# Expert steps of four 32-slot chunks in three column tiles, with two weight copies, loads in expert order and 8 KB runs

## The chip, the cores and the metric

One Trainium2 chip, of which the kernel uses one core. The metric is the time of one execution on the device in microseconds (us), lower is better.

## The reference

One inference step of a two-layer backbone on 640 tokens (128 context tokens, then 512 latent tokens), 1024 wide, all in fp32. Each layer is an adaLN-modulated norm, one input projection, a pooling mixer beside multi-head latent attention, an output projection, and then a mixture of experts, which is what the change is about:

```python
scores = jax.nn.sigmoid(jnp.dot(t, router_w))
sel = scores + router_b
...
a = jnp.einsum('td,edf->tef', t, w_gate)
b = jnp.einsum('td,edf->tef', t, w_up)
act = jax.nn.silu(a) * b * gates[:, :, None]
return jnp.einsum('tef,efd->td', act, w_down)
```

Each token goes to 2 of 16 experts, so there are 1280 token rows per layer. An expert has a gate and an up matrix (1024 x 256) and a down matrix (256 x 1024), 1 MB each, 3 MB (3.146 million bytes) in all; a layer reads all 16. Worked out with the reference's own router on its inputs, the tokens of expert 0 to 15 are:

- layer 0: 75, 62, 61, 88, 132, 151, 152, 137, 29, 56, 52, 65, 54, 41, 60, 65
- layer 1: 103, 72, 81, 108, 100, 66, 83, 119, 56, 70, 40, 70, 85, 50, 93, 84

## The kernel before, in words

**Routing.** After the output projection VectorE (the `vector` block, lines 2154 to 2205) turns the top-2 mask into a list of slots sorted by expert. An expert's rows fill whole chunks of `CH = 64` slots; two chunks make a step of 128 rows. Expert 0 gets at least two chunks, so that step 0 holds expert 0 alone and its row numbers (`idx[:, 0]`, line 2164) are there before the others (`idx[:, 1:]`, line 2184). Chunks are sorted by expert, `fin[e]` is the number of steps after which expert e is done, `ech` and `eslot` hold the expert and the ring place of every chunk.

**A step** (lines 1107 to 1163 on TensorE). GpSimd gathers the step's 128 rows of the normed activations from DRAM into `xg` (line 1642). TensorE transposes them in eight pieces (1090), ScalarE and VectorE copy four pieces each to `xgT` (1445, 2191). `gate_up` multiplies them with the gate matrix and then the up matrix (1120): eight slices of the contraction, and in each of them two matmuls side by side in the array, one for each chunk, 64 columns of the array wide:

```python
for k in range(DC):
    for h in range(2):
        m = mm(dst[CH * h:CH * h + CH, 0:DE], xgT[:, k, CH * h:CH * h + CH],
               weights(h, k * 2 * DE + lo, DE), ...,
               tile_position=(0, CH * h), skip_group_check=True)
```

An fp32 matmul stands in the profile as two records (two passes). ScalarE applies silu (1467), VectorE multiplies the two (2268), TensorE transposes the product (1141) between the transposes of the next step's rows, ScalarE copies it (1470), and the down product follows (1160), again for the two chunks side by side. VectorE scales it with the gate vector (2277, 2289) and ScalarE's queue stores 128 rows to `y_rows` (1482).

**Weights.** They are loaded into a ring of `RING = 5` places of 3 MB (`load_expert`, lines 590 to 600, SP's queue), gate and up as runs of 1 KB (256 numbers of one row), down as runs of 4 KB. Expert 5 and later wait until the expert five before them is done. Chunk 0 of a step reads its weights straight from the ring, at an address held in a register; chunk 1 reads a copy (`half_gu`, `half_d`), since its expert can be another. ScalarE copies half of it (1458, 1462) and VectorE the other half (2218, 2222), three instructions of 1024 columns each on either engine. Each ring place has a semaphore, `ld_w[s]`, and TensorE, ScalarE and VectorE wait on all five of them in every step (1098, 1461, 2221), with values worked out in registers from the expert's number.

**Order around the steps.** On VectorE: rows copy, gate and up copies for the next step, the gate vector, the down copy, the scaling of the step's output. On ScalarE: silu, the two copies of the transposed product, rows copy, gate and up copies, down copy, store. Loads of experts 3 and 4 wait on SP for `r_slot` and `r_gate`, both set by VectorE after the routing (617 to 621). In the last step VectorE first builds the tables that spread the step's output to its tokens (`early_tables`, 2245), for two tiles of tokens in layer 0 and five in layer 1. Then GpSimd gathers the rows of `y_rows` for the tokens (1664), and they are added to x.

Of the kernel before, what the change touches and what calls it, by code (L numbers as in the profile page):

```python
# [52 lines left out]
CH = 64  # L53
NSTEP = 18
NSTEP_MIN = 2 * NTOK // P
NCHUNK = 2 * NSTEP
NSLOT = NSTEP * P
RING = 5
EARLY = [[0, 1], list(range(NT))]
# [29 lines left out]
def constants():  # L89
# [47 lines left out]
    put("chunk", np.tile(np.arange(NCHUNK, dtype=np.float32)[None], (P, 1)))  # L137
    least = np.tile((np.arange(NTOK // CH) * CH).astype(np.float32), (NE, 1))
    least[0, 0:2] = -1
    put("least", np.tile(least.reshape(1, -1), (P, 1)))  # L140
# [4 lines left out]
def step_kernel(nc, x_prompt, x_sample, cache_ckv, cache_krope, c, c_ctx, ada_w, ada_b, norm1_g, norm2_g, w_in, pool_w,  # L145
# [3 lines left out]
    with es:  # L149
# [123 lines left out]
        wgu = [at(6144 * s, DC, 2 * DE) for s in range(RING)]  # L273
        wd = [at(6144 * s + 4096, 2, D) for s in range(RING)]
        half_gu = flat[:, 0:4096]
        half_d = at(30720, 2 * D)

        fin = fin_s[:, :]

        def fifths(n):  # L280
            return (n * 13) >> 6
# [5 lines left out]
        def loads_of(s, e):  # L287

            return fifths(e + (RING + 1 - s if s > 0 else 1)) * 48

        def loads_before(s, l):

            return 48 + l * 48 * sum(slot_of(e) == s for e in range(NE))
# [20 lines left out]
        ecmp = view(big, rt + 1730, (NCHUNK, NE))  # L314
        ecnt = big[:, rt + 3640:rt + 3640 + NCHUNK]
        idx = big[:, 35600:35600 + NSTEP].bitcast(U32)
        ech = big[:, 35620:35620 + NCHUNK].bitcast(I32)
        n_more_s = big[:, 35680:35681].bitcast(I32)
        eslot = big[:, 35690:35690 + NCHUNK].bitcast(I32)
        is_ctx = big[:, 35740:35740 + NSTEP]  # L320
        is_ctx1 = big[:, 35760:35761]
# [18 lines left out]
        def early_rows_of(l, t, w):  # L340
# [8 lines left out]
            return flat[:, (i - 2) * D:(i - 1) * D] if i < 6 else at((i - 6) * D, D)  # L349
# [13 lines left out]
        ctx_bank = [o6, tb5]  # L363

# [29 lines left out]
        ld_w = [sem(f"ld_w{s}") for s in range(RING)]  # L394
# [10 lines left out]
        def lsem(name, count):  # L405
# [34 lines left out]
                                              "gu_mm", "dn_mm", "b_st", "w_a", "w_d")]  # L440
# [18 lines left out]
        def _(sp):  # L459
# [18 lines left out]
            def load_layer(l, expert_done):  # L478
# [19 lines left out]
                if l > 0:  # L498
                    dn_mm, b_st = by_layer[l - 1][10:12]
# [3 lines left out]
                    sp.wait_ge(dn_mm, steps)  # L503
# [25 lines left out]
            for s in range(RING):  # L529
                sp.sem_inc(ld_w[s], 48)  # L530
# [5 lines left out]
            for l in range(DEPTH):  # L536
# [51 lines left out]
                b_t, b_ta, b_td, b_sil, b_act, b_at, b_atc, b_sel, b_yd, gu_mm, dn_mm, b_st, *w_s = by_layer[l]  # L588

                def load_expert(e):  # L590

                    s = slot_of(e)
                    if e >= RING:
                        steps = sp.value_load(fin[0:1, e - RING:e - RING + 1], min_val=1, max_val=NSTEP)
                        sp.wait_ge(gu_mm, steps * 2)
                    sp.dma_start(wgu[s][:, :, 0:DE], w_gate[l, e].rearrange("(k p) n -> p k n", p=P)).then_inc(ld_w[s], 16)
                    sp.dma_start(wgu[s][:, :, DE:2 * DE], w_up[l, e].rearrange("(k p) n -> p k n", p=P)).then_inc(ld_w[s], 16)
                    if e >= RING:
                        sp.wait_ge(dn_mm, steps)
# [1725 lines left out]
```

## Time and profile before

| what | value |
|---|---|
| median of 3 runs | 1113.89 us (1113.77 to 1116.4) |
| span of the profiled execution | 1112.5 us |
| median less that span | 1.4 us |
| TensorE busy | 1058.8 us, 95% of the span |
| granted TensorE clock, mean | 0.998 of 2.4 GHz |
| bytes moved by DMA | 241.47 MB |
| expert steps | 29 (14 in layer 0, 15 in layer 1) |

The profile gives the span from the first to the last instruction. No time of its own stands beside it; the difference to the median is what lies around the span. TensorE's busy time counts overlapping matmuls once; the mean time of one matmul in a list of groups is from its start to its modelled end, and two that run side by side each count in full in their own group. Times in a timeline are from the start of the span. "Idle" stands in square brackets, with what ended it.

### The profile page before, as it was taken

To read this page: it belongs to the slowest core of one execution; us is meant where nothing else is said; L and a number is where in the kernel's file an instruction comes from. 1 tells how busy PE (TensorE), PEld (TensorE's weight loads), DVE (VectorE), ACT (ScalarE), POOL (GpSimd) and SP (SyncE) were. 2 spreads that over 40 slices of the span, in tenths; PEclk is the share of its full clock that TensorE was granted. 3 is DMA by queue.
4 is the path that set the end of the run, shared out by engine and by line. 5 is a ranking of instruction groups with operands and counts; after the bars stand their busy time and mean duration, and the time that the engine had idled before them with its cause. 6 is when DMAs were issued, how large, how long until landed. Compare 5 with 4: busy or idle time off the path is not lost.

```text
span 1112.5 us, 17990 instructions
## 1 busy us (share of the span) xinstructions
PE 1058.8 (95%) x5918; PEld 589.1 (53%) x5919; DVE 572.7 (51%) x1223; ACT 389.0 (35%) x800; POOL 204.8 (18%) x313
## 2 busy tenths in 40 slices
PE   3999999999999899999999999899999979999996
PEld 0566564555544455555546655555644445555552
DVE  0334545665345754454574545476724674534557
ACT  0332224444211244444333222454511134444540
POOL 0133456000000100100152435800000011001003
PEclk9999999999999999999999999999999999999999
DMA  9940006668801799999981000557540379999917
GB/s 351 361 138 1 1 9 238 217 222 302 331 19 40 248 378 377 381 358 366 332 289 41 1 1 0 187 194 279 207 149 38 112 260 376 381 379 380 376 78 284
DMA packets 129064, 241.47 MB, mean 217 GB/s; under 512 B 12304, under 2 KB 92192, under 8 KB 122864
## 3 DMA queue, kind: packets, MB, share of 16 engines
q1 hardware_dynamic: 115904, 194.83, 50.1%
q0 software_dynamic: 7056, 25.69, 6.3%
q10 hardware_dynamic: 6048, 20.22, 4.5%
q8 instruction: 32, 0.52, 0.2%
q14 instruction: 24, 0.20, 0.0%
HBM read 213.63 MB, written 27.10 MB: 216 GB/s over the span
## 4 chain that ended last, share of the span: by engine, by line
PE 80%; DMA 8%; DVE 3%; issue 3%; SPq 3%; POOL 1%; ACT 1%; DVEq 0%; POOLq 0%; ACTq 0%
PE bank L1120 17%; PE pair L1045 12%; PE pair L1160 9%; PE pair L762 7%; PE pair L777 6%; DMA big<-ada_w 4%; PE pair L895 4%; PE pair L794 3%; PE bank L811 3%; PE bank L931 3%; PE bank L672 3%; PE pair L1090 3%; PE bank L910 2%; PE bank L746 2%; DMA big<-y_rows,big 2%
## 5 line engine op out<-in xcount | busy, mean ns | idle before, releaser
L1120 PE MATMUL bank<-big,actT 128*64 (+1 forms) x928 | 206.3, 380 | 2.4 <-ACT actT L1445 1.9
L1120 PE MATMUL bank<-actT 128*64 128x256 f32 x928 | 206.5, 381 | 0.0
L1120 PEld LDWEIGHTS bank<-big,actT 128*64 128x64 f32 x928 | 124.7, 137 | 83.1 <-issue 26.0
L1045 PE MATMUL pair<-big,actT 128*128 128x512 f32 x320 | 142.7, 598 | 0.0
L1120 PEld LDWEIGHTS bank<-actT 128*64 128x64 f32 x928 | 124.7, 137 | 0.0
L1160 PE MATMUL pair<-big 128*64 (+1 forms) x464 | 106.0, 598 | 0.7 <-ACT big L1470 0.7
L1045 PEld LDWEIGHTS pair<-big,actT 128*128 128x128 f32 x320 | 59.0, 190 | 67.8 <-issue 67.6
L762 PE MATMUL pair<-big,actT 128*128 128x384 f32 (+1 forms) x320 | 93.6, 447 | 0.3 <-ACT actT L1218 0.2
L1988 DVE TENSOR_REDUCE mx<-pair 128x1 f32<-128x640 f32 x64 | 52.7, 823 | 72.0 <-PE pair L896 71.9
L1642 POOL DMA_INDIRECT big<-h_rows,big x29 | 27.7, 956 | 304.3 <-PE pair L1090 286.9
L762 PEld LDWEIGHTS pair<-big,actT 128*128 128x128 f32 x320 | 59.5, 190 | 29.3 <-ACT actT L1218 1.9
L895 PE MATMUL pair<-big 96*128 96x512 f32 x128 | 70.7, 634 | 1.1 <-PE bank L672 0.7
L672 PE MATMUL bank<-big,condT 128*32 128x512 f32 x384 | 53.0, 634 | 18.8 <-DMA big<-ada_w 18.7
L777 PE MATMUL pair<-actT,big 128*128 128x512 f32 (+1 forms) x256 | 70.9, 434 | 0.0
L1458 ACT ACTIVATE actT<-big 128x1024 f32 x54 | 54.1, 1049 | 37.3 <-DMA big<-w_gate 13.8
L2268 DVE TENSOR_TENSOR big<-big,bank 128x128 f32<-128x128 f32 x58 | 14.1, 284 | 102.9 <-PE bank L1120 102.9
L1631 POOL TENSOR_SCALAR ss<-big 128x1 f32<-128x1 f32 x10 | 3.0, 302 | 345.0 <-ACT big L1403 345.0
L1160 PEld LDWEIGHTS pair<-big 128*64 128x64 f32 x464 | 30.9, 136 | 55.3 <-issue 55.3
L2218 DVE COPY actT<-big 128x1024 f32 x54 | 35.0, 690 | 45.7 <-DMA big<-w_gate 17.0
L1467 ACT ACT_TABLE_LOAD x27 | 34.6, 1283 | 68.0 <-DVE big L2289 68.0
L1345 ACT ACTIVATE big<-pair,nmax 128x640 f32<-128x640 f32 x64 | 50.9, 795 | 19.0 <-DVE nmax L1991 18.6
L777 PEld LDWEIGHTS pair<-actT,big 128*128 128x128 f32 x256 | 39.1, 191 | 29.7 <-issue 29.7
(274 smaller groups left out, 1628.9 us busy)
## 6 DMA issues: line engine op xcount, KB each, us to landing
big<-ada_w SPq DMA_DIRECT2D x48, 1024.0 KB, 5.0
big<-w_gate SPq DMA_DIRECT2D x32, 1024.0 KB, 13.1
big<-w_up SPq DMA_DIRECT2D x32, 1024.0 KB, 16.3
big<-w_down SPq DMA_DIRECT2D x32, 1024.0 KB, 14.5
y_rows<-big ACTq DMA_DIRECT2D x28, 512.0 KB
big<-w_out SPq DMA_DIRECT2D x4, 2048.0 KB, 13.4
big<-mod_rows SPq DMA_DIRECT2D x16, 512.0 KB, 9.2
h_rows<-big ACTq DMA_DIRECT2D x10, 512.0 KB, 2.7
```

The costliest lines, as they stand in the source:

```text
L672: m = mm(a7[32 * j:32 * j + 32, :], condT[:, k, :], w[:, j, :], start=(k == 0), stop=(k == DC - 1), tile_position=(0, 32 * j), skip_group_ ...
L762: m = mm(in_bank(t)[:, to:to + n], actT[:, k, t * P:(t + 1) * P], vw.win_q[:, k, lo:lo + n], start=(k == 0), stop=(k == DC - 1))
L777: m = mm(pair[0][:, to:to + cols], vw.win_p[:, k, g * P:(g + 1) * P], actT[:, k, t0:t0 + cols], start=(k == 0), stop=(k == DC - 1))
L895: mm(dst[:, 0:HALF], q, vw.kT[0:QH, h, 0:HALF], start=True, stop=True)
L1045: m = mm(dst, actT[:, k, t * P:(t + 1) * P], vw.wo[n][:, k, :], start=(k == order[0]), stop=(k == order[-1]))
L1120: m = mm(dst[CH * h:CH * h + CH, 0:DE], xgT[:, k, CH * h:CH * h + CH], weights(h, k * 2 * DE + lo, DE), start=(k == 0), stop=(k == DC - 1) ...
L1160: m = mm(pair[1][CH * h:CH * h + CH, j * HALF:(j + 1) * HALF], acT[:, k, CH * h:CH * h + CH], weights(h, 4096 + k * D + j * HALF, HALF), s ...
L1345: f(prob[un % 4][:, :, :], score_bank(un)[:, 0:NLK * P].rearrange("p (k n) -> p k n", n=P), ACT.Exp, bias=nmax[:, un % 2:un % 2 + 1], scal ...
L1458: return f(pieces(half_gu), pieces(slot[:, 0:4096]), ACT.Copy)
L1467: f(sil, tb4[:, 0:DE], ACT.Silu).then_inc(b_sil, 1)
L1988: link(v.tensor_reduce(mx[:, un % 2:un % 2 + 1], score_bank(un)[:, 0:NLK * P], AX.X, ALU.max))
L2218: return v.tensor_copy(pieces(half_gu), pieces(slot[:, 0:4096]))
```

## The change

- A chunk has 32 slots, a step four chunks. Every expert gets at least one chunk, every expert with an odd number at least two, expert 0 at least four. The steps are worked as three column tiles, `TILES = [(0, 64), (64, 32), (96, 32)]`: two chunks of one expert that stand next to each other share the 64-slot tile, the other two chunks get 32 slots each. Which chunks these are is worked out on VectorE (`tile_e`), and slots are moved within their step so that the pair comes first.
- The 64-slot tile reads the ring. The tile at 64 reads a copy made by ScalarE alone, the tile at 96 one made by VectorE alone. Each copy is six pieces of 1024 columns a step, in three buffers per engine; one semaphore, `used`, counts the pieces that TensorE has used (six a step).
- Step 0 is one tile of 128 slots, read from the ring, with no copies. TensorE makes the list of the other rows (`list_rows`) inside step 0, after its first piece.
- `load_expert` loads gate and up as 8 KB runs (partition p takes rows 8p to 8p+7); the normed rows are written in the matching order (`by_row`, a stride of 128 numbers). Each of gate, up and down has one semaphore, and a load waits until the same matrix of the expert before has landed.
- The buffers that receive the last gathers of layer 1 move, and one wait of GpSimd in the last step of layer 1 goes.
- The loop is peeled: step 0, then the loop, then the last step.

```diff
-CH = 64
-NSTEP = 18
+CH = 32
+NSTEP = 19
+TILES = [(0, 64), (64, 32), (96, 32)]
...
     least = np.tile((np.arange(NTOK // CH) * CH).astype(np.float32), (NE, 1))
-    least[0, 0:2] = -1
+    least[:, 0] = -1
+    least[1::2, 1] = -1
+    least[0, 0:FIRST_CHUNKS] = -1
...
                 def load_expert(e):
                     s = slot_of(e)
                     if e >= RING:
                         steps = sp.value_load(fin[0:1, e - RING:e - RING + 1], min_val=1, max_val=NSTEP)
-                        sp.wait_ge(gu_mm, steps * 2)
-                    sp.dma_start(wgu[s][:, :, 0:DE], w_gate[l, e].rearrange("(k p) n -> p k n", p=P)).then_inc(ld_w[s], 16)
...
+                        sp.wait_ge(used, used_in(steps, 1))
+                    if e > 0:
+                        sp.wait_ge(ld_wg, landed(l, e - 1))
+                    sp.dma_start(wg[s], w_gate[l, e].rearrange("(p k) n -> p (k n)", k=DC)).then_inc(ld_wg, 16)
...
+                def products(n, land, place, first):
+                    tiles = [(0, P)] if first else TILES
+                    pe.wait_ge(b_ta, n + 1)
+                    pe.wait_ge(b_td, n + 1)
+                    for i in range(4):
+                        if first and i == 1:
+                            list_rows()
+                        weights = weights_of(n, i, land, place, first)
+                        dst = (tb4, tb5)[i // 2]
+                        for k in range(4 * (i % 2), 4 * (i % 2) + 4):
+                            for c, (lo, m_) in enumerate(tiles):
+                                m = mm(dst[lo:lo + m_, 0:DE], xgT[:, k, lo:lo + m_], weights(c, k % 4 * DE, DE),
+                                       start=(k == 0), stop=(k == DC - 1), tile_position=(0, lo), skip_group_check=True)
+                        m.then_inc(used, 1)
...
```

ScalarE's step, and VectorE's:

```diff
+                def step(n, first, last):
+                    if not first:
+                        part = part_place(n)
+                        part_copy_w(n, part, 3)
+                    act.wait_ge(used, used_at(n, 1))
                     f(sil, tb4[:, 0:DE], ACT.Silu).then_inc(b_sil, 1)
+                    if not first:
+                        part_copy_w(n, part, 4)
+                        part_copy_w(n, part, 5)
                     for k in range(2):
                         act.wait_ge(b_at, n * 2 + (k + 1))
                         f(acT[:, k, :], (o6, a7)[k][:, 0:P], ACT.Copy).then_inc(b_atc, 1)
...
+                    rows_copy(n + 2)
+                    part = part_place(n + 1)
+                    for i in range(3):
+                        part_copy_w(n + 1, part, i)
```

```diff
+                def step(n, first, last):
                     if last:
                         early_tables()
+                    if not first:
+                        part = part_place(n)
+                        for i in range(3, NPIECES):
+                            part_copy_w(n, part, i)
                     ve.wait_ge(b_sil, n + 1)
```

GpSimd's gathers at the end of a layer:

```diff
-                        if i == (2 if l == 0 else 6):
-                            reached(dn_mm, n_steps)
+                        if i == 2 and l == 0:
+                            reached(used, used_in(n_steps, 5))
```

The routing chain on VectorE gets 15 more instructions before the slots are known and 13 more between them and `r_slot`.

## Rows read from the trace of the kernel before

**Rows 1.** The page, parts 1 and 2: busy times; 40 slices of the span

```profile
PE 1058.8 (95%) x5918; PEld 589.1 (53%) x5919; DVE 572.7 (51%) x1223; ACT 389.0 (35%) x800; POOL 204.8 (18%) x313
...
DMA  9940006668801799999981000557540379999917
```

**Rows 2.** The page, part 5: gathers of rows, one for each step

```profile
L1642 POOL DMA_INDIRECT big<-h_rows,big x29 | 27.7, 956 | 304.3 <-PE pair L1090 286.9
```

**Rows 3.** Chain of waits, in order of time: start, length, what

```profile
400.32 6.97 PE bank L1120 x64
408.66 3.65 PE pair L1160 x16
412.32 7.10 PE bank L1120 x64
```

**Rows 4.** Stretches: busy PE, PEld, DVE, ACT, POOL, PE clock, DMA share, GB/s

```profile
12.00:27.00 15.00, 8.38 (x52) 2.10 (x44) 0.76 (x1) 1.15 (x2) 0.76 (x2) 0.89 1.00 417
387.40:557.40 170.00, 168.10 (x1253) 95.02 (x1254) 81.08 (x149) 76.98 (x108) 14.21 (x15) 1.00 1.03 366
908.50:1091.40 182.90, 180.26 (x1343) 101.74 (x1344) 90.02 (x168) 83.31 (x118) 17.32 (x19) 1.00 0.91 325
400.00:538.00 138.00, 137.74 (x1036) 77.84 (x1036) 64.72 (x104) 65.83 (x91) 10.33 (x11) 1.00 1.05 373
```

**Rows 5.** Timeline of TensorE from one step into the next: start, length, what

```profile
406.90 0.38 PE L1120 MATMUL bank<-big,actT 128*64 x1
406.92 0.38 PE L1120 MATMUL bank<-actT 128*64 128x256 f32 x1
407.23 0.55 PE L1090 MATMUL pair<-cst,big 128*128 128x128 f32 x3
...
411.71 0.60 PE L1160 MATMUL pair<-big 128*64 x2
412.29 0.42 PE L1120 MATMUL bank<-big,actT 128*64 x1
...
412.55 0.38 PE L1120 MATMUL bank<-big,actT 128*64 x1
```

**Rows 6.** The page, part 5: gate and up copies on ScalarE and VectorE

```profile
L1458 ACT ACTIVATE actT<-big 128x1024 f32 x54 | 54.1, 1049 | 37.3 <-DMA big<-w_gate 13.8
...
L2218 DVE COPY actT<-big 128x1024 f32 x54 | 35.0, 690 | 45.7 <-DMA big<-w_gate 17.0
```

**Rows 7.** Timelines around step 0 of layer 0: VectorE, GpSimd, SP, TensorE

```profile
379.45 0.24 DVE L2167 TENSOR_TENSOR big<-big,mask 128x80 f32<-128x80 f32 x1
...
384.80 0.75 DVE L2187 TENSOR_REDUCE big<-big 128x36 f32<-128x576 f32 x1
...
386.54 0.69 DVE L2191 COPY actT<-pair 128x512 f32<-128x512 f32 x1 [0.98 <-PE pair L1090]
...
387.26 0.95 POOL L1642 DMA_INDIRECT big<-h_rows,big  x1 [6.08 <-PE pair L1090]
...
390.86 0.37 SPq L596 DMA_DIRECT2D big<-w_gate  x1
...
395.43 0.55 PE L1090 MATMUL pair<-cst,big 128*128 128x128 f32 x3 [0.86 <-DMA big<-h_rows,big]
```

**Rows 8.** Timeline of VectorE in the last step of layer 0, then of layer 1

```profile
548.61 0.14 DVE L2247 TENSOR_SCALAR big<-fin 128x1 f32<-128x1 int32 x1
...
550.43 0.49 DVE L2257 TENSOR_TENSOR part_s<-part_s,bias_s 128x128 f32<-128x128 f32 x2
...
1081.00 1.22 DVE L2289 TENSOR_TENSOR big<-pair,big 128x1024 f32<-128x1024 f32 x1
1082.13 0.14 DVE L2247 TENSOR_SCALAR big<-fin 128x1 f32<-128x1 int32 x1
...
1086.33 0.28 DVE L2257 TENSOR_TENSOR big<-big 128x128 f32<-128x128 f32 x1
```

**Rows 9.** Timeline of VectorE: the last normed rows of layer 0

```profile
371.29 1.29 DVE L2151 SCALAR_TENSOR_TENSOR big<-big,rs 128x1024 f32<-128x1024 f32 x1 [0.59 <-POOL rs L1632]
```

More of the change, by code:

```diff
@@ L393, in step_kernel @@
         mod_st = sem("mod_st")
-        ld_w = [sem(f"ld_w{s}") for s in range(RING)]
+        ld_wg, ld_wu, ld_wd = sem("ld_wg"), sem("ld_wu"), sem("ld_wd")
         y_fill = sem("y_fill")
@@ L1107, in products @@
[L1107 to L1123 removed]
+                    land = pe.value_load(eland[0:1, bass.ds(n, 1)], min_val=16, max_val=landed(DEPTH - 1, NE - 1))
@@ L1133, in products @@
-                    return weights
-                def rest(n, last, weights):
-                    w_a, w_d = w_s
+                    for i in range(4):
[8 more added lines that the diff above has]
+                        m.then_inc(used, 1)
@@ L1139, in turn_act, with rest @@
+                def rest(n, land, place, first, last):
+                    tiles = [(0, P)] if first else TILES
                     def turn_act(k):
@@ L1170, in _ @@
                 n_more = pe.value_load(n_more_s[0:1, 0:1], min_val=NSTEP_MIN - 1, max_val=NSTEP - 1)
-                rest(0, False, weights)
+                rest(0, land_0, place_0, True, False)
                 def step(n, last):
-                    rest(n, last, products(n))
+                    land, place = load_place(n)
+                    products(n, land, place, False)
+                    rest(n, land, place, False, last)
                 with pe.Fori(1, n_more) as i:
@@ L1499, in _ @@
                 act.wait_ge(op_mm, L(op_mm) + 2 * NT)
[L1500 to L1504 removed]
+                act.sem_inc(w_a, NPIECES - 1)
                 rows_copy(1)
                 act.wait_ge(y_fill, 16 * (NSTEP - NSTEP_MIN))
[L1507 to L1508 removed]
+                step(0, True, False)
                 n_more = act.value_load(n_more_s[0:1, 0:1], min_val=NSTEP_MIN - 1, max_val=NSTEP - 1)
[L1510 to L1514 removed]
+                with act.Fori(1, n_more) as i:
+                    step(i, False, False)
+                step(n_more, False, True)
         @block.gpsimd
@@ new lines, in _ @@
+                link(red(ecnt, ecmp, AX.X, ALU.add))
+                ts(fin, ends, float(FIRST_CHUNKS - 1), None, ALU.add)
+                link(ts(ecnt, ecnt, float(NE - 1), None, ALU.min))
+                ve.wait_ge(r_pe1, L(r_pe1) + 2)
+                v.tensor_copy(idx[:, 1:NSTEP], pair[1][:, 1:NSTEP]).then_inc(r_idx, 1)
+                ts(is_ctx, pair[1][:, 0:NSTEP], float(SEQ), None, ALU.is_lt).then_inc(b_yd, 1)
+                e0, e1, e2, e3 = (ecnt.rearrange("p (n j) -> p n j", j=FIRST_CHUNKS)[:, :, j] for j in range(4))
@@ L2289, in step @@
                     tt(yb, pair[1][:, :], yb, ALU.mult).then_inc(b_yd, 1)
-                with ve.Fori(0, n_more) as i:
-                    step(i, False)
-                step(n_more, True)
+                    part_copy_w(n + 1, part, 2)
+                step(0, True, False)
+                with ve.Fori(1, n_more) as i:
+                    step(i, False, False)
+                step(n_more, False, True)
             l = DEPTH - 1
```

331 lines of the change are left out of this document (173 added, 158 removed).

## The prediction, made blind

> **What bounds the kernel now.** I read the busy times of the page first: TensorE is busy for 95% of the span, and the DMA digits are 9 or near it in slices 15 to 20 and again in the second mixture of experts [rows 1]. So either could be the limit there. The chain of waits settles it: from step to step it is only TensorE's own matmuls, 7.1 us of gate and up (L1120), 3.6 us of down (L1160), and the transposes between [rows 3]. From the gate and up product at 400.32 to that at 412.32 is 12.0 us; between the stretches of the next view it is 12.1 us a step. The gathers count 29 steps [rows 2], 14 in layer 0 (170.0 us) and 15 in layer 1 (182.9 us) [rows 4]. No step is longer than another but the first of a layer, where TensorE waits 0.86 us for gathered rows [rows 7]. Yet the DMA share of steady steps in layer 0 is 1.05 at 373 GB/s [rows 4]: the queues are full all the time and the weights come just in time. A change that shortens the steps' total has to bring the bytes sooner as well.
>
> **Fewer steps.** With the reference's token counts, 64-slot chunks give 28 and 29 chunks, so 14 and 15 steps, which is what the gathers show. Chunks of 32 with the new minima give 48 and 49, four to a step: 12 and 13. Four steps of 12.1 us go: -48.4 us, if a step costs what it did.
>
> **What a step costs.** Its arithmetic on TensorE is as before if the three tiles run side by side as the two do now: the two chunks' matmuls start 0.02 us apart and each takes 0.38 [rows 5]. I take that; the other case is the first rival. At the seam TensorE's next product starts 0.58 us after the last pair of the down product [rows 5], which streams for 0.43 (eight pairs in 3.65 us, the last 0.60 long, [rows 3, 5]): 0.15 us are left, in which its queue works out the five waits on `ld_w`. One wait replaces them, so up to 23 x 0.15 = 3.4 us come back. Against it stand the copies. ScalarE now copies six pieces of 1.05 us instead of three, VectorE six of 0.69 [rows 6], 6.3 and 4.1 us a step. By ScalarE's order (silu, pieces 4 and 5, then the transposed product) the latter comes some 8.5 us after the step's start, when the down product wants it: up to 0.2 us late, 4.6 us over 23 steps. I take the two at nothing together, and both ends for the range. VectorE has over 1 us to spare for each piece.
>
> **The bytes.** From the load of expert 3 at 390.9 [rows 7] thirteen experts remain (40.9 MB), and a gather and a store (1.05 MB together) for each step. Before, at 373 GB/s, 54.5 MB take 146 us and end at 537; expert 15 is needed at 545. After, `r_slot` and `r_gate` come about 5 us later, expert 15 is needed at 387.4 + 11 x 12.1 + 2 = 522.5, and 52.4 MB at 373 GB/s would end at 536.5: 14 us late. The 8 KB runs decide. While the kernel starts, `ada_w` is loaded in runs of 8 KB, at 417 GB/s [rows 4]; two thirds of the weights would go at that rate, and 52.4 MB at some 410 take 128 us and end at 523.7. I take 0.5 us a layer for what is late, 1 us in all; the ends are 0 and 14 us a layer. The Trainium skill (DMA: Bandwidth & Descriptors, Where 436 GB/s comes from) holds that the core's share of HBM, about 358 GB/s, binds such loads; by that rule the longer runs would bring nothing and the 14 us a layer stand. The rows of this trace are above it at either run length.
>
> **Step 0 of each layer.** It starts no later: what step 0 needs comes ahead of the added instructions. The gather for step 1 does. Before, it starts at 387.26, when the transposes free the buffer [rows 7]. After, VectorE's comparison and reduction over 76 chunks instead of 36 (0.75 us each for 576 numbers, so 1.4 each for 1216, [rows 7]) follow the rows copy, and TensorE makes the list only after the first piece (389.2 to 389.8): the list's copy comes at about 390.6, 3.4 us later. The fewer loads in flight give perhaps 1.4 us back: +2.0 us for each layer, 0.3 to 3.5. The fifteen added routing instructions (some 0.25 us where one waits for the last, [rows 7]) take about 2.5 us, beside the transposes and the first piece.
>
> **The last step of each layer.** VectorE builds the tables from 1082.13 to 1086.6 in layer 1, 4.5 us, and in 2.3 us in layer 0 [rows 8]. Now they stand ahead of its pieces 3 to 5, of which TensorE wants piece 3 5.1 us after the step starts. VectorE is free about 3.1 us after it (the output's scaling, 1.22 us, [rows 8], and piece 2), then come the tables, two register loads and the copy: 9.2 us in layer 1, 7.2 in layer 0. TensorE waits 4.0 and 2.0 us. In layer 1 some 1.2 us hide in waits of the final additions: +4.8 in all, 2 to 7.
>
> **The rest.** The normed rows are written at a stride of 512 bytes; the last such instruction, 1.29 us, stands before the last mask [rows 9]. The trace has none with such a stride: at least 0, at most twice the time there and in its half before, 2 us a layer. I take 0, since VectorE's time here goes by the count of its numbers (1.29 us for 1024, 0.75 for 576, [rows 7, 9]). The gathers at the end of layer 1 lose a wait, but VectorE's additions bound that stretch: 0. One count per matrix keeps at most three transfers in flight; three of 1 MB cover 7 us at 417 GB/s: 0.
>
> **Sum:** -48.4 + 1 + 4 + 4.8 = -38.6. The profiled span, 1112.5, becomes 1073.9; the median of the runs is 1.4 above its span: **1075.3 us**. Own range: -3.4 with the low ends (0, 0.6 and 2) gives 1065, taken as 1063 for the rounding of 25 steps; the high ends (7, 7, 4.6, 4 for the strides, and half of the 28 us of late bytes) give 1102.
>
> **Rival 1, slower: the tiles of 64 and 32 columns exclude each other.** Wherever the width of the matmuls changes, the next starts later than where it stays: the last pair of L1120 starts at 406.90 and 406.92, and pairs follow each other every 0.21 us (64 records in 7.10, [rows 3]), but the full-width transpose behind it starts after 0.31 [rows 5]: 0.10 us for one change. Where that is a wait for the array to be empty, the 64-column tile can't share it with the 32-column ones. Then the 16 products of gate and up and the 4 double ones of down each run twice in turn: +10.3 us a step, 40 changes of 0.10 us, and 1.5 us for weights not loaded ahead (the first pair takes 0.26 instead of 0.21, [rows 5]): +15.8, times 23 steps (step 0 has one tile) +363. The waits of the first and last steps hide in it (-8): 1430 us. It decides from 1.7 us a step (38.6 over 23), so one change of 0.10 in each of 20 groups would do. For it: the delay at every change. Against: every change in this trace is between tiles that overlap in the array, which must wait anyway; tiles that don't overlap start together. The Trainium skill has the rule (TensorEngine Tiling (Array Packing), Key Properties): changing the tiling mode, not just the tile, drains TensorE. By it this rival holds; the 0.10 us agree, but no row mixes widths in disjoint columns.
>
> **Rival 2, slower: they overlap, but each change costs its 0.10 us.** 3.8 us a step, 23 steps: 1075 + 87 = 1162.
>
> **Rival 3: the longer runs bring nothing,** and expert 15 is 14 us late in each layer. 1075.3 - 1 + 28 = 1102 us. For it: the rate rose in part because the start has no gathers. Against: 417 beside 373 GB/s.
>
> **Chances.** As forecast 0.58; rival 3 0.06; within 0.3% (3.3 us, about what a measurement of this kernel tells from no change), by several waits together, 0.02; rival 1 0.30; rival 2 0.04. Both signs hold much, so the range goes from 1063 to the end of rival 1, 1440; the likeliest case's own is 1063 to 1102. Faster 0.64, same 0.02, slower 0.34.
>
> **What would show it.** 25 gathers; steady steps of 12.0 to 12.3 us; three matmuls of a group starting within 0.03 us of each other, against 0.5 us for rival 1. `w_gate` and `w_up` landing sooner with a DMA share under 1 and no copies waiting for them after the tenth step; the second gather some 3 us later; a wait of TensorE for VectorE's piece 3 in the last steps. A step of 14 us or more would make the prediction wrong at its root.

## The result, and the profile after

The changed kernel takes **1429.27 us** (1427.26 to 1432.43, 4 runs), the kernel before in the same comparison 1115.03 us (1113.77 to 1116.4, 4 runs): 1.2814 times the time, 95% interval 1.2788 to 1.284. The forecast was 1075.3 us and faster. What came is rival 1, which gave 1430 us with a chance of 0.30.

The page's parts 1 and 2, its gathers, and the two stretches of the experts (columns as in [rows 4]):

```profile
PE 1370.2 (96%) x6402; PEld 590.8 (41%) x6403; DVE 624.4 (44%) x1312; ACT 404.2 (28%) x810; POOL 201.7 (14%) x309
...
DMA  9900166850597324563440015661069444644115
...
L1676 POOL DMA_INDIRECT big<-h_rows,big x25 | 23.9, 955 | 549.1 <-PE pair L1129 511.3
```

```profile
388.40:705.70 317.30, 313.34 (x1483) 93.35 (x1484) 98.86 (x182) 87.45 (x114) 13.33 (x13) 1.00 0.52 194
1060.10:1405.80 345.70, 342.07 (x1613) 102.24 (x1614) 110.03 (x204) 95.81 (x126) 20.13 (x21) 1.00 0.46 172
```

The change does what it says: 25 gathers for 29 [rows 2]. The DMA queues, full before [rows 4], are half empty. The two stretches got longer, 317.3 us for 170.0 and 345.7 for 182.9, and TensorE is busy all through them (313.3 us for 168.1, and 342.1 for 180.3). VectorE and ScalarE, which now copy more, grew by some 10 to 20 us in each and stand idle for most of it. The chain of waits shows each step alike:

```profile
404.10 18.11 PE bank L1165 x96
423.57 7.94 PE pair L1192 x24
431.51 18.11 PE bank L1165 x96
```

From one gate and up product (L1165) to the next it is 27.4 us where it was 12.1 on average (12.0 in [rows 3]): 18.1 for 7.1, and the down product (L1192) 7.9 for 3.65. Between them it is 1.36 us (422.21 to 423.57), as before. The timeline of TensorE inside a product shows where that goes (start, length; "x3" are three records in a row):

```profile
412.52 0.40 PE L1165 MATMUL bank<-actT 128*32 128x256 f32 x1
412.53 0.40 PE L1165 MATMUL bank<-big,actT 128*32 128x256 f32 x1
412.76 0.38 PE L1165 MATMUL bank<-actT 128*32 128x256 f32 x1
412.77 0.95 PE L1165 MATMUL bank<-big,actT 128*32 128x256 f32 x3
413.65 0.40 PE L1165 MATMUL bank<-actT 128*32 128x256 f32 x1
413.66 0.40 PE L1165 MATMUL bank<-big,actT 128*32 128x256 f32 x1
```

The same in the weight loads (PEld):

```profile
413.08 0.19 PEld L1165 LDWEIGHTS bank<-big,actT 128*64 128x64 f32 x2 [0.41 <-issue]
413.65 0.11 PEld L1165 LDWEIGHTS bank<-actT 128*32 128x32 f32 x1 [0.39 <-issue]
```

The two tiles of 32 columns start 0.01 us apart, as close as the two of 64 in [rows 5]. The tile of 64 is the last two of the "x3" records of 412.77, which the weight loads of 64 columns date: it starts at 413.08, and nothing of another width does until 413.65. A group takes 1.13 us (412.52 to 413.65); two equal tiles take 0.43.

What the change made late is small beside it. TensorE's waits in step 0 of layer 0 (us in all, times, the longest):

```profile
PE pair L1129 <- DMA big<-h_rows,big: 2.9, 1, 2.9
PE bank L1165 <- ACT actT L1481: 0.9, 1, 0.9
PE bank L1175 <- DVE big L2337: 0.3, 1, 0.3
```

### The profile page after: what moved, and what is told of

Its sections match the earlier page's. It is cut to its first block, busy times and chain, and to the rows that moved or that the text cites. A ratio compares the mean times of both kernels' runs of the same rounds, so it can differ in the third digit from the quotient of the medians.

```text
span 1425.4 us, 19416 instructions
## 1 busy us (share of the span) xinstructions
PE 1370.2 (96%) x6402; PEld 590.8 (41%) x6403; DVE 624.4 (44%) x1312; ACT 404.2 (28%) x810; POOL 201.7 (14%) x309
## 4 chain that ended last, share of the span: by engine, by line
PE 87%; DMA 5%; DVE 4%; issue 2%; SPq 1%; ACT 1%; POOL 0%; DVEq 0%; ACTq 0%; POOLq 0%
PE bank L1165 29%; PE pair L1192 13%; PE pair L1081 10%; PE pair L798 6%; PE pair L813 5%; DMA big<-ada_w 4%; PE pair L931 3%; PE bank L708 3%; PE pair L830 3%; PE bank L847 3%; PE bank L967 3%; PE bank L946 2%; PE pair L1129 2%; PE bank L782 1%; DMA big<-h_rows,big 1%
## 5 line engine op out<-in xcount | busy, mean ns | idle before, releaser
L1165 PE MATMUL bank<-big,actT 128*64 (+2 forms) x1168 | 341.8, 399 | 1.7 <-ACT actT L1481 1.7
L1165 PE MATMUL bank<-actT 128*32 128x256 f32 x1104 | 229.0, 391 | 0.0
L1497 ACT ACTIVATE actT<-big 128x1024 f32 x138 | 145.5, 1056 | 270.0 <-PE bank L1165 155.7
L1192 PE MATMUL pair<-big 128*32 128x512 f32 (+2 forms) x384 | 191.9, 612 | 0.7 <-ACT big L1511 0.7
L1165 PEld LDWEIGHTS bank<-big,actT 128*64 128x64 f32 (+2 forms) x1168 | 107.4, 129 | 164.8 <-issue 161.2
L2289 DVE COPY big<-big 128x1024 f32 x92 | 63.6, 691 | 180.1 <-PE bank L1165 173.0
L1165 PEld LDWEIGHTS bank<-actT 128*32 128x32 f32 x1104 | 51.8, 108 | 141.6 <-issue 141.6
L1192 PE MATMUL pair<-actT,big 128*32 128x512 f32 x184 | 96.2, 605 | 0.0
L1192 PEld LDWEIGHTS pair<-big 128*32 128x32 f32 (+2 forms) x384 | 33.4, 125 | 65.6 <-issue 65.6
L2357 DVE TENSOR_TENSOR big<-pair,big 128x1024 f32<-128x1024 f32 x23 | 28.1, 1224 | 68.4 <-PE pair L1192 68.4
L1381 ACT ACTIVATE big<-pair,nmax 128x640 f32<-128x640 f32 x64 | 50.8, 794 | 18.9 <-DVE nmax L2026 18.5
```

What stands on the lines that cost most here:

```text
L1165: m = mm(dst[lo:lo + m_, 0:DE], xgT[:, k, lo:lo + m_], weights(c, k % 4 * DE, DE), start=(k == 0), stop=(k == DC - 1), tile_position=(0, l ...
L1192: m = mm(pair[1][lo:lo + m_, j * HALF:(j + 1) * HALF], acT[:, k, lo:lo + m_], weights(c, j * HALF, HALF), start=(k == 0), stop=(k == 1), t ...
L1381: f(prob[un % 4][:, :, :], score_bank(un)[:, 0:NLK * P].rearrange("p (k n) -> p k n", n=P), ACT.Exp, bias=nmax[:, un % 2:un % 2 + 1], scal ...
L1497: f(parts[1][i % 3], slot[:, i * PIECE:(i + 1) * PIECE], ACT.Copy).then_inc(w_a, 1)
L2289: v.tensor_copy(parts[2][i % 3], slot[:, i * PIECE:(i + 1) * PIECE]).then_inc(w_d, 1)
```

## The experiments

In the timings of a run, the kernel before stood beside it on the same chip (medians 1114 to 1117 us). Single profiles of kernels that are alike outside the expert steps differ by up to 6 us in the start and the end, so terms of a few us are read from the stretches of the experts, first product to last.

### Which of the costs of the mix it is

**Four tiles of one width.** The changed kernel, with a list of tiles of TensorE's own (source of the weights, first column, columns) in place of `TILES`:

```diff
+MM_TILES = [(0, 0, 32), (1, 32, 32), (1, 64, 32), (2, 96, 32)]
...
-                            for c, (lo, m_) in enumerate(tiles):
+                            for c, lo, m_ in tiles:
```

> The changed kernel with the pair of chunks as two tiles of 32 columns, so that all four tiles of a step have one width. The tile at 32 reads ScalarE's copy, so slots 32 to 63 are multiplied with the weights of the third chunk's expert: the time is meant, the output of those slots is left wrong. Theory (tiles of different widths exclude each other, tiles of one width don't): the four stream side by side, gate and up take 7.1 us a step again, down 3.65, the step 12.1 to 12.5, the whole 1075 to 1090 us. Rival A (it is the number of matmuls and weight loads that costs: six records of a group take 1.13 us, so eight take 1.5): the step about 34 us, the whole about 1580 us. Rival B (tiles of 32 columns are slow by themselves): no better than now, 1429 us.

Measured: 1092.5 us (1091.41 to 1094.34), 0.978 of before (0.974 to 0.9821). The timeline inside a product (the first line is the tile that reads the ring, the second the other three):

```profile
952.81 0.38 PE L1166 MATMUL bank<-big,actT 128*32 x1
952.82 0.39 PE L1166 MATMUL bank<-actT 128*32 128x256 f32 x3
953.03 0.38 PE L1166 MATMUL bank<-big,actT 128*32 x1
953.03 0.39 PE L1166 MATMUL bank<-actT 128*32 128x256 f32 x3
```

Four tiles start within 0.02 us, and every 0.21 us. Splitting the wide tile in two, with more matmuls, took 337 us off. Both rivals fall: it is neither the number of matmuls nor the narrow tiles. The time is 2.5 us above the theory's own range, which the next run takes up.

**Two tiles of 64.** The same list with `[(0, 0, 64), (1, 64, 64)]`.

> The changed kernel with the third and fourth chunk as one tile of 64 columns on ScalarE's copy (slots 96 to 127 are multiplied with the third chunk's weights, so that part of the output is left wrong; VectorE's copies are still made and waited for). Theory: with one width the rest of the sum is measured as it was forecast: steps of 12.0 to 12.3 us and 1063 to 1102 us, 1075 by the sum. Rival (the copies, the step's waits or the loads of the changed kernel cost as well, hidden now behind the long steps): steps of over 12.5 us with TensorE waiting in them, over 1102 us.

Measured: 1080.38 us (1078.13 to 1080.71). One thing has to be added: with wrong weights in layer 0 the tokens of layer 1 choose other experts, which fill 12 steps there, not 13 (24 gathers in all; the run with four tiles has 25). One step more makes it 1092.7, the four tiles' time. So two widths of tile give one time. Both are 17 us above the forecast, and all steps but the first of the loop are 12.2 us or longer. The theory's range holds, and its steps of 12.0 to 12.3 us hold for most of layer 1; but the rival has a point too: something of the changed kernel costs TensorE time beyond the widths, though less than the rival said (over 12.5 us a step, over 1102 us).

**Fewer changes of width.** The changed kernel's three tiles, in another order:

```diff
-                        for k in range(4 * (i % 2), 4 * (i % 2) + 4):
-                            for c, (lo, m_) in enumerate(tiles):
+                        for cs in ([0], [1, 2])[:len(tiles)]:
+                            for k, c in [(k_, c_) for k_ in range(4 * (i % 2), 4 * (i % 2) + 4) for c_ in cs if c_ < len(tiles)]:
+                                lo, m_ = tiles[c]
...
```

> The changed kernel with the matmuls of a piece in another order: all of the 64-column tile first, then all of the two 32-column ones; the same matmuls with two changes of width in a piece where there were eight (two where there were four in a piece of the down product). Theory (exclusion and a drain at each change): the exclusion stays, 14.4 us for gate and up at least, but 24 + 4 changes with some 0.1 us and weights not loaded ahead go: gate and up 14.5 to 15 us, down 7.3 to 7.6, the step 23 to 24, the whole 1330 to 1350 us. Rival (only changes of width cost, tiles of both widths can overlap): gate and up about 8 us, the whole about 1115 us. Rival (exclusion alone costs and changes nothing): 1429 us as now.

Measured: 1343.87 us (2 runs), 1.2024 of before, as the theory said. From its chain of waits:

```profile
431.69 14.89 PE bank L1166 x96
...
447.95 7.40 PE pair L1194 x24
455.35 14.89 PE bank L1166 x96
```

The step is 23.66 us. A step of the changed kernel has 40 changes of width, this one 12 (two in each of six pieces): 27.42 - 23.66 = 3.76 us for 28 changes, 0.134 us for each, with the weights that aren't loaded ahead. The two products give the same price by themselves: 18.11 - 14.89 us for 24 changes, 7.94 - 7.40 for four. What is left above a step of equal tiles (11.87, below) is 11.8 us, of which 12 changes are 1.6; **10.2 us is the exclusion**, each group run twice in turn.

**The mix alone, in the kernel before.** Chunk 1 as two tiles of 32 columns on the same copy:

```diff
+MM_TILES = [(0, 0, 64), (1, 64, 32), (1, 96, 32)]
...
-                            for h in range(2):
+                            for h, a, w_ in MM_TILES:
...
```

> The kernel before with chunk 1 worked as two tiles of 32 columns on the same copy (the same products, nothing else changed). Theory: the mix of widths alone makes the steps long: each of the 29 steps takes 27.4 us instead of 12.1, 1114 + 29 x 15.3 = 1558 us, less a few hidden waits, 1545 to 1560. Rival (the length comes from the new waits, the three copies or the counting of pieces): 1114 us, or up to 1130 with a few more instructions to issue.

Measured: 1558.57 us (2 runs), inside the theory's 1545 to 1560; the rival falls. Its chain shows the same two numbers, with nothing else of the change in it:

```profile
442.76 18.11 PE bank L1121 x96
462.24 7.94 PE pair L1161 x24
```

### What else the forecast had missed

**ScalarE's piece 3.** In the run with two tiles of 64, TensorE waits for ScalarE's copies 15 times, 5.6 us in all. Part of the chain of waits into such a wait ("ACTq" is the queue of ScalarE at work on loads of registers, issues and jumps):

```profile
942.03 1.23 DVE big L2358
...
943.41 0.35 ACTq L1524
...
944.10 0.28 ACTq L1488
...
944.71 0.36 ACTq L1489
...
945.52 1.07 ACT actT L1498
946.58 0.13 issue
946.71 1.95 PE bank L1166 x16
```

VectorE's scaling of the output (L2358) is done at 943.3. Then ScalarE issues the store (L1524), jumps to the head of its loop, loads two registers (L1488, L1489), and only at 945.52 copies piece 3. TensorE goes on at 946.71. The next run moves that copy behind the store:

```diff
-                        part_copy_w(n, part, 3)
...
                     act.dma_start(y_rows[bass.ds(n * P, P), :], yb).then_inc(b_st, 16)
+                    part_copy_w(n + 1, part, 3)
```

> The kernel with two tiles of 64 columns (1080 us), and ScalarE copies piece 3 of the next step at the end of the step, behind the store, with the registers it has, in place of behind the loop's jump and two register loads. In the trace of two tiles of 64, ScalarE's piece 3 starts 1.8 us after the store was issued and ends just after TensorE wants it; steady steps of layer 1 are 12.3 us where the first loop step is 11.9. Theory (piece 3 on ScalarE is the term that my sum of a step lacks): steps of 11.9 to 12.0 us in layer 1, 0.3 to 0.4 us less in each of some 21 steps, 1072 to 1075 us. Rival (something else, weights or VectorE's pieces, is as late): under 2 us gained.

Measured: 1070.9 us (1068.07 to 1072.77), 9.5 less, with 24 gathers as its base. That is a little more than the theory gave, and the rival falls. All steps between the third and the last are 11.87 us, in both layers:

```profile
936.65 6.91 PE bank L1166 x64
...
944.93 3.58 PE pair L1193 x16
948.52 1.50 PE bank L1166 x13
```

**The 8 KB runs.** On that kernel, for gate and up alike, and with the normed rows written without a stride again:

```diff
-                    sp.dma_start(wg[s], w_gate[l, e].rearrange("(p k) n -> p (k n)", k=DC)).then_inc(ld_wg, 16)
+                    sp.dma_start(wg[s].rearrange("p (k n) -> p k n", k=DC), w_gate[l, e].rearrange("(k p) n -> p k n", p=P)).then_inc(ld_wg, 16)
...
```

> The kernel with two tiles of 64 and the early piece 3 (1070.9 us), and gate and up loaded in runs of 1 KB again, with the normed rows written without a stride. Theory (by my sum the longer runs bring the bytes sooner: 417 GB/s against 373): weights come late towards the end of a layer, 10 to 14 us a layer with the shorter runs, 1085 to 1099 us; and the DMA share of a steady stretch of layer 0 rises to 1. Rival (the rate goes by the memory, not by the length of the runs, or the queues have that much to spare): within 2 us of 1070.9.

Measured: 1091.29 us (1088.46 to 1093.46), 20.4 more. A stretch of layer 0, first in runs of 8 KB, then of 1 KB (columns as in [rows 4]):

```profile
413.80:500.00 86.20, 86.02 (x646) 47.91 (x646) 54.84 (x88) 54.55 (x74) 7.50 (x8) 1.00 1.02 420
```

```profile
413.80:500.00 86.20, 86.16 (x644) 47.43 (x640) 53.18 (x84) 54.68 (x72) 7.03 (x8) 1.00 1.06 379
```

Both keep the queues full, and carry 420 and 379 GB/s (the gathers and stores of the steps are in both). The short runs come late from the tenth step of the layer on; what TensorE waits for there is VectorE's copy, which waits for `w_gate` (one of the four waits, 1.9 us, is the last step's, which is another matter):

```profile
PE bank L1166 <- DVE actT L2290: 11.5, 4, 6.2
```

The rival falls. The three late steps of layer 0 are 13.5 us longer in all than 11.87 us each, the four of layer 1 11.2 us. That is more than the 9.6 us that TensorE waits for copies there in layer 0: the step behind the wait of 6.2 us is 2.5 us longer with no wait of its own, and TensorE's granted clock is at the lower of its two levels, 1.2 GHz, as that step starts (0.52 of full speed from 521 to 528). And that a load waits for the same matrix of the expert before it costs nothing that shows: the queues are full with it.

### A version that is right and faster

Making the wide tile two tiles of 32 isn't enough: in all kernels so far the one tile that reads the ring at an address held in a register is the one at column 0, so the tile at column 32 needs its expert's weights from elsewhere. Two ways were tried.

**A branch.** TensorE's step stands five times in the program, once for each place of the ring:

```diff
+                    for s in range(RING):
+                        with pe.If(place == s):
+                            products(n, land, slice(s, s + 1), False)
+                            rest(n, land, slice(s, s + 1), False, last)
```

> The changed kernel with four tiles of 32 columns, and the whole computation as it should be: TensorE's step stands five times in the program, once for each place of the ring, and a branch on the register picks one, so that the two tiles of the pair read the ring at fixed addresses. Theory (one width is all that was missing, and a branch costs little more than the register loads): steps of 12.3 to 12.8 us, 1090 to 1105 us in all, faster than the kernel before. Rival (TensorE's queue has to fetch the taken copy of the step, and stands still meanwhile): 1 to 2 us more in each of 23 steps, 1115 to 1140 us, no gain over before.

Measured: 1607.64 us (2 runs): both theory and rival are far off. The chain, where the place changes:

```profile
431.81 9.04 DMA big<-w_gate
440.86 23.18 issue
464.04 8.68 PE bank L1166 x128
```

The weights are there at 440.86, and TensorE starts 23.2 us later with nothing in the profile to wait for. Such "issue" makes 24.9% of the whole chain, and steps take 18 to 49 us. Behind such a halt the products are slow as well: 8.7 us at a granted clock of 0.81 (464.0 to 472.7) where the run below takes 6.9 at 1.00. The queue for instructions, here and in the run below:

```profile
q8 instruction: 226, 3.70, 1.1%
```

```profile
q8 instruction: 34, 0.56, 0.2%
```

That speaks for a fetch of the program behind each jump: 192 transfers more for 25 steps, in each of which the queue passes over four copies. The next step's product begins 4.3 us behind the end of the step; by the reference's tokens that step is expert 4's, whose place is 0 and whose copy stands first in the loop. The fetch wasn't measured apart, so this cause is argued and not shown.

**The pair in the middle.** The single chunk of the ring stands in slots 0 to 31, and both tiles of the pair read ScalarE's copy:

```diff
...
+link(ts(slot_a[:, :], slot_i[:, :], CH, 1, ALU.bitwise_and, ALU.logical_shift_left))
+link(ts(slot_a[:, :], slot_a[:, :], 2 * CH, None, ALU.bitwise_xor))
+link(tt(slot_i[:, :], slot_i[:, :], slot_a[:, :], ALU.bitwise_xor))
...
-tt(tile_e[:, 0, :], e1, to_a, ALU.add)
-tt(tile_e[:, 1, :], e2, to_b1, ALU.add)
+tt(tile_e[:, 1, :], e1, to_a, ALU.add)
+tt(tile_e[:, 0, :], e2, to_b1, ALU.add)
```

> Four tiles of 32 columns with every slot's own weights, and no branch: the pair of chunks stands in the middle of the step (slots 32 to 95) and both its tiles read ScalarE's copy; the single chunk in slots 0 to 31 reads the ring, the one in 96 to 127 VectorE's copy. Three more instructions on VectorE swap chunks 0 and 2 in the slot numbers. ScalarE's piece 3 is copied behind the store as in the run before. Theory (one width, and the two terms found so far): steps of 12.1 to 12.2 us in layer 1, 1076 to 1086 us, faster than before by 3%. Rival (four tiles cost more than two by their number: in the first run with four tiles the gate and up product took 7.33 to 7.5 us, two tiles 7.13): steps of 12.4 us or more, over 1088 us.

Measured: 1087.74 us (1086.19 to 1088.95), 0.9763 of before (0.9747 to 0.978), the whole computation, 25 gathers. Steady steps are 11.87 us, below both expectations, so the rival falls; the time is just above the theory's range:

```profile
446.93 6.91 PE bank L1166 x128
...
455.23 3.57 PE pair L1193 x32
458.80 1.27 PE bank L1166 x21
```

So the number of tiles costs nothing. The rest is in the first and last steps; two runs go there, each with its own edit on top of this kernel.

> The run with the pair in the middle, and in step 0 of each layer TensorE makes the list of rows ahead of the first product (while the rows are copied), VectorE takes it over ahead of its comparisons for the chunks, and VectorE works out the gate values behind the step's product in place of ahead of it. Theory (in step 0 two things are late: the rows of step 1 by 1.5 us, and then VectorE's product, behind its longer routing, by 1.7): the wait for the rows goes and the other with it, 2 to 3.2 us less in each layer, 4 to 6.5 in all against the run with the pair in the middle. Rival (the time goes to what comes next, the weights' copies for step 1 or loads that start later): under 2 us gained.

> The run with the pair in the middle, and in the last step of each layer VectorE builds the early tables in two parts: the first between its pieces 4 and 5, the second behind the product, in place of both ahead of piece 3. Theory (the tables ahead of the pieces hold TensorE up): last steps take 12.2 to 13 us in place of some 16 to 17, 3 to 4 us less in each layer, 6 to 8 in all against the run with the pair in the middle. Rival (the end of layer 1 is bound by VectorE's additions, so that what TensorE gains there is waited out behind it): only layer 0 gains, 3 to 4 us in all.

The excerpt shows the move of the list, which is of the step 0 edit, and the split of the tables, which is the last-step edit; the step 0 edit's new order on VectorE is not in it:

```diff
+                    if first:
+                        list_rows()
                     pe.wait_ge(b_ta, n + 1)
...
-                        if first and i == 1:
-                            list_rows()
...
                     if not first:
                         part = part_place(n)
                         for i in range(3, NPIECES):
+                            if last and i == NPIECES - 1:
+                                early_tables()
                             part_copy_w(n, part, i)
...
+                    if last:
+                        late_tables()
```

Measured: step 0, 1080.04 us (0.9694, 0.9674 to 0.9713); last step, 1077.55 us (0.9665, 0.9648 to 0.9681). Both gain more than their theories gave, 7.7 us for 4 to 6.5 and 10.2 for 6 to 8. By the stretches of layer 0 and 1, the pair in the middle takes 154.5 and 167.3 us, with the step 0 edit 149.1 and 166.1, with the last-step edit 150.3 and 161.1. VectorE in the last step of layer 1, without the edit:

```profile
1049.03 0.14 DVE L2316 TENSOR_SCALAR big<-fin 128x1 f32<-128x1 int32 x1
...
1053.19 0.28 DVE L2326 TENSOR_TENSOR big<-big 128x128 f32<-128x128 f32 x1
1054.05 0.86 DVE L2293 COPY actT<-big 128x1024 f32 x1 [0.58 <-issue]
```

Piece 3, wanted 5.35 us into the step that begins at 1046.39, is there at 1054.9. With the edit the last steps take 12.0 us for 15.9 and 19.6.

A wait costs more than its own length here. TensorE waits 3.4 us for that piece, but the last step of layer 1 is 7.7 us longer than 11.87. Most of the rest goes with the granted clock. It is 1.00 in steady steps; behind TensorE's wait for piece 3, and behind its waits for rows and product in step 0 of layer 0, it is at 1.2 GHz, the lower of its two levels (the two lines are the pair in the middle; the third number from the end is the clock):

```profile
403.00:409.00 6.00, 5.83 (x13) 3.25 (x14) 3.53 (x7) 2.74 (x5) 0.94 (x1) 0.50 1.01 422
...
1054.00:1064.00 10.00, 8.09 (x54) 2.81 (x58) 5.08 (x8) 1.07 (x4) 4.15 (x4) 0.51 0.47 145
```

In the first stretch matmuls of the down product follow each other every 0.85 us where they do every 0.43 at 2.4 GHz. With the step 0 edit that step runs at 1.00 and takes 13.75 us for 18.5, with the last-step edit the last steps run at 1.00. So either edit takes away more than the waits that it aims at.

But from the last product to the end of the span, where VectorE adds the rows up, it is 19.7 us without the last-step edit and 25.4 with it (21.5 in the last run below, which has it too): of the 6.1 us that layer 1 gains, 1.8 to 5.7 are given back, for which the rival stands. Against it stands the timing, 10.2 us better, which is the gain of both layers (4.1 and 6.1) with nothing given back. The profiled execution was the slowest of its four (1080.31 us), so its 25.4 may be long for this kernel; how much is given back stays open.

Both edits together, and then the normed rows written without a stride (`by_row` changes with the line below):

> The pair in the middle with both edits, those of step 0 and those of the last step. Theory (they are in different stretches and add up): 1087.7 less 7.7 less 10.2, 1070 us, 1066 to 1074. Rival (the step 0 edit only moves the same late bytes, of which the queues have none to spare at 417 GB/s, so that they come back as waits in the last third of a layer): 1074 to 1078 us, no better than the last-step edit alone.

> The run before this one, and VectorE writes the normed rows without a stride; TensorE's transposes of the gathered rows take every eighth column in place of 128 neighbouring ones, which gives the same order for the 8 KB runs. In the trace of the changed kernel a strided instruction of 1024 numbers takes 2.0 us on VectorE where a plain one takes 1.28, and the mask is ready 1.5 us later. Theory (I forecast nothing for the strides, and they cost about 1 us on the path of each layer): 1.5 to 3 us less than the run before, and transposes as long as they were (0.21 to 0.27 us each). Rival (TensorE pays for the stride as VectorE did): eight transposes a step get longer by half, 0.8 us or more a step, 15 us or more slower.

```diff
-m = tr(pair[0][:, k * P:(k + 1) * P], xg[:, k * P:(k + 1) * P], ident)
+m = tr(pair[0][:, k * P:(k + 1) * P], xg.rearrange("q (p k) -> q k p", k=DC)[:, k, :], ident)
```

Measured: both, 1076.03 us (0.964, 0.9621 to 0.966); without the stride, **1072.97 us** (1069.16 to 1074.45), **0.9618** of before (0.9598 to 0.9637). The two edits don't add up in the timing (11.7 us for 7.7 and 10.2), and the time is in the rival's range; with both, TensorE waits twice, 2.9 us in all, for VectorE's copy of a piece, with the queues full (share 1.02 at 416 GB/s from 405 to 520). The last step down, 3.1 us, is at the upper end of the theory, but the two intervals overlap, and by the stretches of the two layers the runs are equal (147.6 and 159.1 us, 147.6 and 159.2). The rival, a transpose longer by half, falls. What is clear is the price of the stride: on VectorE, the same instruction with the stride and without it,

```profile
L2188 DVE SCALAR_TENSOR_TENSOR big<-big,rs 128x1024 f32<-128x1024 f32 x2 | 4.0, 1993 | 0.8 <-POOL rs L1667 0.8
```

```profile
L2188 DVE SCALAR_TENSOR_TENSOR big<-big,rs 128x1024 f32<-128x1024 f32 x2 | 2.6, 1284 | 1.2 <-POOL rs L1667 1.2
```

and on TensorE, the transposes without a stride and with it:

```profile
L1130 PE MATMUL pair<-cst,big 128*128 128x128 f32 x200 | 33.4, 279 | 2.7 <-DMA big<-h_rows,big 2.7
```

```profile
L1130 PE MATMUL pair<-cst,big 128*128 128x128 f32 x200 | 35.0, 287 | 2.9 <-DMA big<-h_rows,big 2.9
```

VectorE loses 0.71 us for an instruction of 1024 numbers, TensorE 8 ns for a transpose.

## Why the prediction was wrong

**The step that failed** is "its arithmetic on TensorE is as before if the three tiles run side by side ... I take that". They don't. The forecast argued that every change of width in the trace lay between tiles that overlap in the array, and took the case that no row showed. The rows had the number that speaks for the rival, 0.10 us at each change [rows 5], and one change in each of 20 groups was said to be enough to turn the sign. What came in its place: tiles of the two widths run in turn, 10.2 us a step, and each of 40 changes of width costs 0.134 us, 5.4 us a step. The Trainium skill (TensorEngine Tiling (Array Packing), Key Properties) says that changing the tiling mode, not just the tile, drains TensorE. The traces agree for disjoint columns too: runs with one width, of 32 or of 64, have none of it, and the kernel before gets all of it from the mix alone. With rule and rows on one side and an absence of rows on the other, 0.30 was too little for it.

**Rival 1's own sum.** A step was to cost 15.8 us more; it cost 15.3 (27.42 for 12.1), or 15.6 over a step of equal tiles in this kernel (11.87). Its exclusion, 10.3, measured 10.2; its 40 changes and late weights, 5.5 together, measured 40 x 0.134 = 5.4. That the time came out within 1 us is in part luck: the base to which the steps were added was 17 us too low, the steps 0.5 us too long, 12 us over 23, and the long steps hid more than the 8 us that were taken off. Rival 2 counts 3.8 us a step for the same changes; with the 40 of rival 1 it is 4.0, and its time 1167 us in place of 1162.

**The base.** With one width the changed kernel takes 1092.5 us, 17 above the forecast and inside its own range. Term by term:

- **Fewer steps**: 25, as counted.
- **The seam and the copies**, taken as nothing together with 0 to 0.2 us a step for late copies. The seam is as forecast: from the last pair of the down product to the next product it is 0.43 us for 0.58. Some 0.1 us more is gained at the first pair of the product and ahead of the down product, so that a step is 11.87 for 12.1 once nothing else is late; that the one wait for five does it was not tested apart. The copies cost more: the forecast looked at pieces 4 and 5 and missed piece 3, whose copy stands behind the store, the loop's jump and two register loads. Steady steps of layer 1 were 12.3 for 11.87, and the early copy took 9.5 us off the whole. It counted instructions on the engine and not what its queue does between them.
- **The bytes**: right in kind and size. 8 KB runs carry 420 GB/s (410 taken), 1 KB runs 379 (373 taken). The steps of a layer that come late are longer by 13.5 and 11.2 us where 14 a layer was forecast; in the timing the short runs cost 20.4 us where 27 was the forecast's difference, but that run has no stride to pay for either. Rival 3 falls. The Trainium skill (DMA: Bandwidth & Descriptors, Where 436 GB/s comes from) has about 358 GB/s as the limit of such loads. The measurement decides: with one core at work, as here, both rates are above it, and the 8 KB run's loads and gathers without its stores still are (374 GB/s).
- **Step 0**: +2.0 us each was forecast. In the changed kernel the first step is 2.9 and 3.4 us longer (15.63 and 16.57 for 12.73 and 13.15), inside the range of 0.3 to 3.5. The wait for rows grew from 0.86 [rows 7] to 2.9, which is the 2.0; the rest is the list's matmuls and waits of 0.9 and 0.3 us for copies and products. In layer 1 the granted clock is at 1.2 GHz behind that wait (0.50 from 1071 to 1073). In the version with the pair in the middle it is 5.8 and 3.9. There VectorE's product comes 1.1 and 2.0 us late behind its routing instructions, which the forecast had put at nothing, and in layer 0 the clock is down from 403 to 409, which is some 2.1 us for the five matmuls of the down product that take 0.85 us.
- **The last step**: hidden in the changed kernel, as rival 1 said. With one width and the early piece 3, last steps took 16.3 and 16.9 us for 11.87: 4.4 and 5.0 longer. The mechanism was as described: TensorE waits for VectorE's piece 3 behind the tables, 2.4 us in layer 0 and 3.4 in layer 1 where 2.0 and 4.0 were forecast. What the sum had nothing for is the granted clock behind the wait, which falls to 1.2 GHz in either last step (0.57 over 532 to 536 and over 1040.5 to 1044.5). The kernel before has no such stretch in its experts' steps, so no row told what a wait costs there.
- **The strided writes**: forecast 0, since VectorE's time seemed to go by the count of its numbers. They cost 0.7 us an instruction of 1024 numbers. The last mask before the slots was used 1.55 us later in layer 0 (378.79 for 377.24), inside the upper bound of 2, but VectorE was already 0.88 us later ahead of the last strided rows (361.40 for 360.52), so that these account for 0.7.

## What to carry to other kernels

In every run here tiles of 64 and of 32 columns ran in turn, and tiles of one width side by side: before columns are split unevenly, split the wide tile into equal ones, which costs nothing in this kernel, and choose which tile reads what so that the operand with a register address stays at column 0, as in these kernels. When copies or loads move to another place in a loop, follow the engine's queue as well (issues, jumps, register loads): 1.8 us of it stood between ScalarE's store and its next copy. When you price a wait of TensorE, look at the granted clock behind it too: a wait of 3.4 us made a step 5.0 us longer in one kernel and 7.7 in another. Where a layout needs a stride, try it on TensorE's reads before VectorE's writes: 8 ns a transpose stand against 0.71 us an instruction here.

## What the runs showed of the hardware that was not expected

- Tiles of 64 and of 32 columns in disjoint columns run in turn, and a change costs 0.134 us (40 against 12 of them in a step).
- Behind waits of 2.4 and 3.4 us TensorE's granted clock was 1.2 GHz for some us, and matmuls of the down product followed every 0.85 us for 0.43.
- A branch of TensorE to another copy of its step cost 23.2 us of "issue" at the one looked at, with the instruction queue moving 3.70 MB instead of 0.56.
- A write with a stride of 512 bytes takes 2.0 us on VectorE for 1.28 (1024 fp32 numbers), a transpose that reads at a stride of 32 bytes 287 ns for 279.
- With runs of 8 KB in place of 1 KB for two thirds of the weights, full queues carry 420 GB/s for 379.
